# Cross attention's scores as three products of high and low parts, and the memory's values in another buffer

## The reference, cut to what matters

```python
kv = (mem @ mem_w_kv).astype(jnp.float32)
mem_k = kv[..., :D_MODEL].reshape(B, MEM_LEN, XATTN_HEADS, XATTN_HD)   # 4 heads of 256
mem_v = kv[..., D_MODEL:].reshape(B, MEM_LEN, XATTN_HEADS, XATTN_HD)

def memory_cross_attn(x, mem_k, mem_v, wq, wo):
    B, S, _ = x.shape
    q = (x @ wq).reshape(B, S, XATTN_HEADS, XATTN_HD).astype(jnp.float32)
    s = jnp.einsum('bshd,bmhd->bhsm', q, mem_k) * (XATTN_HD ** -0.5)
    p = jax.nn.softmax(s, axis=-1)
    o = jnp.einsum('bhsm,bmhd->bshd', p, mem_v).reshape(B, S, D_MODEL).astype(x.dtype)
    return o @ wo
```

## Time and profile before

| | us |
|---|---|
| median of 3 runs (960.96 to 961.74) | 961.36 |
| the profiled execution, whole | 960.98 |
| its span, first to last instruction | 959.2 |
| PE busy (share of the span) | 945.3 (99%) |
| DVE busy | 685.8 (72%) |
| ACT busy | 518.3 (54%) |
| POOL busy | 54.6 (6%) |
| mean granted TensorE clock, as a share of full speed | 0.997 |

### The profile page before, as it was taken

The page is one execution under the profiler, slowest core; times in us unless marked ns, Lnnn a source line. Parts: engine busy times, 40 slices in busy tenths (PEclk is TensorE's granted clock), DMA queues, the critical chain, the costliest instruction groups (busy, mean ns, idle before and its releaser), DMA issues.

```text
span 959.2 us, 12959 instructions
## 1 busy us (share of the span) xinstructions
PE 945.3 (99%) x5054; PEld 810.4 (84%) x5054; DVE 685.8 (72%) x932; ACT 518.3 (54%) x732; POOL 54.6 (6%) x96
## 2 busy tenths in 40 slices
PE   8999999999999999999999999998999999999996
PEld 8889888888888888888788888887988888888885
DVE  6956578658888775975788777668678886556555
ACT  6756563536655555264275555547465575444543
POOL 0000121001000002100100000002100000000000
PEclk9999999999999999999999999999999999999998
DMA  9975275527988886183289898764631565655521
GB/s 322 337 253 176 88 268 204 209 88 256 338 278 294 283 295 204 52 314 125 88 317 333 271 306 288 249 221 131 229 132 45 176 225 192 219 176 191 178 71 45
DMA packets 110028, 203.00 MB, mean 212 GB/s; under 512 B 4188, under 2 KB 76144, under 8 KB 106640
## 3 DMA queue, kind: packets, MB, share of 16 engines
q1 hardware_dynamic: 106656, 189.67, 58.4%
q0 software_dynamic: 3168, 12.24, 3.7%
q10 hardware_dynamic: 144, 0.26, 0.1%
HBM read 201.09 MB, written 1.06 MB: 211 GB/s over the span
## 4 chain that ended last, share of the span: by engine, by line
PE 90%; DVE 6%; ACT 2%; issue 1%; POOL 0%; DMA 0%; POOLq 0%; SPq 0%; DVEq 0%; ACTq 0%
PE WB L360 20%; PE YB L385 11%; PE YB L378 10%; PE YB L393 10%; PE WB L363 10%; PE YB L439 4%; PE WB L378 2%; PE WB L342 2%; PE WB L385 2%; PE WB L393 2%; PE WB L349 2%; PE WB L345 2%; PE WB L694 1%; PE WB L713 1%; PE WB L477 1%
## 5 line engine op out<-in xcount | busy, mean ns | idle before, releaser
L1709 DVE TENSOR_TENSOR wl<-raw,wh 128x2048 fp32r<-128x2048 f32 (+1 forms) x146 | 334.3, 2297 | 117.4 <-ACT wh L1101 115.1
L1101 ACT CAST wh<-raw 128x2048 fp32r<-128x2048 f32 (+1 forms) x150 | 285.2, 1905 | 30.5 <-PE YB L439 8.9
L360 PE MATMUL WB<-XS,wh 128*128 128x512 f32 x832 | 208.1, 392 | 0.0
L360 PEld LDWEIGHTS WB<-XS,wh 128*128 128x128 f32 x832 | 152.2, 188 | 29.1
L363 PEld LDWEIGHTS WB<-XS,wl 128*128 128x128 f32 x832 | 113.5, 190 | 8.2
L363 PE MATMUL WB<-XS,wl 128*128 128x256 f32 x832 | 116.0, 282 | 0.0
L378 PE MATMUL YB<-wh,FHT 128*128 128x512 f32 x352 | 109.0, 391 | 0.0
L385 PE MATMUL YB<-wl,FHT 128*128 128x512 f32 x352 | 108.6, 390 | 0.0
L393 PE MATMUL YB<-wh,FLT 128*128 128x512 f32 x352 | 108.5, 389 | 0.0
L1275 ACT COPY U<-WB 128x256 f32<-128x256 f32 x102 | 33.0, 376 | 132.8 <-PE WB L363 132.8
L385 PEld LDWEIGHTS YB<-wl,FHT 128*128 128x128 f32 x352 | 66.1, 188 | 14.1
(11 more groups left out here) (338 smaller groups left out, 1205.2 us busy)
## 6 DMA issues: line engine op xcount, KB each, us to landing
raw<-in_mlp_w SPq DMA_DIRECT2D x64, 1024.0 KB, 5.2
raw<-in_w_ada_t SPq DMA_DIRECT2D x24, 1024.0 KB, 5.1
raw<-in_mlstm_w_in SPq DMA_DIRECT2D x11, 1024.0 KB, 8.0
raw<-in_w_ffn_down SPq DMA_DIRECT2D x11, 1024.0 KB, 4.9
raw<-in_w_ffn_gate SPq DMA_DIRECT2D x10, 1024.0 KB, 5.4
raw<-in_w_ffn_up SPq DMA_DIRECT2D x10, 1024.0 KB, 5.6
raw<-in_mem_w_kv SPq DMA_DIRECT2D x8, 1024.0 KB, 5.1
raw<-in_xattn_wq SPq DMA_DIRECT2D x8, 1024.0 KB, 7.2
```

Source lines behind the costliest of these rows:

```text
L360: e.matmul(W[:, :], H[:, at(k)], XS[:, k, :], start=k == 0, stop=False)
L1101: f = e.copy(w[:, 0:a * b], raw[:, 0:a * b])
L1709: f = e.tensor_tensor(L[:, 0:a * b], raw[:, 0:a * b], H[:, 0:a * b].bitcast(F32), ALU.subtract)
```

## The change

Keys are kept as a high part `KH` and a low part `KL_` in a float32r buffer `KHL` (same place in memory as `KV`, which the second block still uses under its own name), queries as high parts in `FH` and low parts in `FL`. `scores(h)` on PE is, for each of the two halves of tokens, two matmuls of high query x high key, two of high x low, and, after a wait for the query's low part, two of low x high. For this

- ACT's copy of a key block becomes a cast into `KH` (same size), and DVE gets four subtractions `key_low(0)` to `key_low(3)`, which now free the key blocks' banks in ACT's place;
- ACT's copies of queries 0 and 1 become casts into `FH`, and for heads 2 and 3 there is a new cast `high(h)`; DVE gets four subtractions `query_low(0)` to `query_low(3)` in each layer;
- the memory's values go to another part of the buffer `AR`, and two vectors (`BV[2]`, `BV[3]`: gain and shift of a later norm) move out of their way; PE's wait for the values moves from `scores` to `values`.

```diff
--- before.py
+++ after.py
@@ -179,13 +179,16 @@
         S = sb("S", [128, 8, 256])
         XS = sb("XS", [128, 8, 512], F32R)
         XH, XL = XS[:, :, 0:256], XS[:, :, 256:512]
+
+        with nc.sbuf_tensor("KHL", [128, 4096], F32R) as KHL:
+            pass
         KV = sb("KV", [128, 4096])
         FHT = sb("FHT", [128, 1280], F32R)
         FLT = sb("FLT", [128, 1280], F32R)
         AR = sb("AR", [128, 8800])
         FH = [FHT[:, 512 * i:512 * i + 512] for i in range(2)]
         FL = [FLT[:, 512 * i:512 * i + 512] for i in range(2)]
-        BV = [sb(f"bv{i}", [128, 1024]) for i in range(2)] + [AR[:, 1024:2048], AR[:, 2048:3072]]
+        BV = [sb(f"bv{i}", [128, 1024]) for i in range(2)] + [AR[:, 4096:5120], AR[:, 5120:6144]]
         IDN = sb("IDN", [128, 128])
         PC = sb("PC", [128, 248])
         SM = sb("SM", [128, 416])
@@ -229,11 +232,11 @@
 
         CT = [S[:, 2 * n:2 * n + 2, :].rearrange("p k c -> p (k c)") for n in range(2)]
 
-        KT = KV[:, 0:2048].rearrange("p (k c) -> p k c", k=8)
-        VM = KV[:, 2048:4096].rearrange("p (t c) -> p t c", t=2)
+        KH, KL_ = (KHL[:, 2048 * n:2048 * n + 2048].rearrange("p (k c) -> p k c", k=8) for n in range(2))
+        VM = AR[:, 2048:4096].rearrange("p (t c) -> p t c", t=2)
 
         TMP = AR[:, 6144:8800]
-        QT = [TMP[:, 512 * n:512 * n + 512] for n in range(2)] + [U[:, 0, 512 * n:512 * n + 512] for n in range(2)]
+        QT = [None, None] + [U[:, 0, 512 * n:512 * n + 512] for n in range(2)]
 
         PART = [U[:, 1, 512 * n:512 * n + 512] for n in range(2)] * 2
         PB = [TMP[:, 1024 + 512 * n:1536 + 512 * n] for n in range(2)]
@@ -686,13 +689,18 @@
 
                 def scores(h):
                     W = bank(("xs", i, h))
-                    e.wait_ge(*act_mlstm["mv", 1, 1])
-                    e.wait_ge(*(act_xa if h < 2 else dve_xa)["q", i, h])
-                    Q = halves(QT[h])
+                    e.wait_ge(*dve_mlstm["mk", 3])
+                    e.wait_ge(*act_xa["qh", i, h])
+                    H, L = halves(FH[h % 2]), halves(FL[h % 2])
                     for t in range(2):
+                        o, tk = W[:, 256 * t:256 * t + 256], slice(128 * t, 128 * t + 128)
                         for f in range(2):
-                            p = e.matmul(W[:, 256 * t:256 * t + 256], Q[:, f, 128 * t:128 * t + 128],
-                                         KT[:, 2 * h + f, :], start=f == 0, stop=f == 1)
+                            e.matmul(o, H[:, f, tk], KH[:, 2 * h + f, :], start=f == 0, stop=False)
+                        for f in range(2):
+                            e.matmul(o, H[:, f, tk], KL_[:, 2 * h + f, :], start=False, stop=False)
+                        e.wait_ge(*dve_xa["ql", i, h])
+                        for f in range(2):
+                            p = e.matmul(o, L[:, f, tk], KH[:, 2 * h + f, :], start=False, stop=f == 1)
                     p.then_inc(pe_xa.add(("s", i, h)))
 
                 def turned(h):
@@ -707,6 +715,7 @@
 
                 def values(h):
                     W = bank(("xv", i, h))
+                    e.wait_ge(*act_mlstm["mv", 1, 1])
                     e.wait_ge(*act_xa["pt", i, h])
                     for d in range(2):
                         for m in range(2):
@@ -720,7 +729,7 @@
                             lambda t, k: e.wait_ge(*dve_xa["o", i, h]))
 
                 def free(t, nb):
-                    return act_xa["q" if t else "ct", i, nb]
+                    return dve_xa["ql", i, nb] if t else act_xa["ct", i, nb]
 
                 s_ = f"wo{i}"
                 pair(s, [("wq", i, 0), ("wq", i, 1)], pe_xa, lambda n: dve_ln["u", s, 0, n])
@@ -1176,8 +1185,7 @@
                 hi_to(M["mk", j] + 3)
                 W = bank_of.get(("mk", j), WB[0])
                 e.wait_ge(*pe_mlstm["mk", j])
-                e.copy(KT[:, 2 * j:2 * j + 2, :], halves(W[:, :])).then_inc(act_mlstm.add(("mk", j)))
-                freed["mk", j] = act_mlstm["mk", j]
+                e.copy(KH[:, 2 * j:2 * j + 2, :], halves(W[:, :])).then_inc(act_mlstm.add(("mk", j)))
 
             def head_a(h):
                 D = DT[h % 2]
@@ -1290,9 +1298,14 @@
                     if h < 2:
                         W = bank_of.get(("xq", i, h), WB[0])
                         e.wait_ge(*pe_xa["xq", i, h])
-                        e.copy(QT[h], W[:, :]).then_inc(act_xa.add(("q", i, h)))
+                        e.copy(FH[h], W[:, :]).then_inc(act_xa.add(("qh", i, h)))
                     else:
                         part(("xq", i, h), PART[h], pe_xa["xq", i, h], act_xa, ("part", i, h))
+
+                def high(h):
+                    e.wait_ge(*dve_xa["q", i, h])
+                    e.wait_ge(*pe_xa["s", i, h - 2])
+                    e.copy(FH[h % 2], QT[h]).then_inc(act_xa.add(("qh", i, h)))
 
                 def scores(h):
                     W, w = bank_of.get(("xs", i, h), WB[0]), cols(("xs", i, h), 6)
@@ -1325,9 +1338,11 @@
                 q(2)
                 hi_to(M["wq", i, 3] + 3)
                 scores(0)
+                high(2)
                 q(3)
                 turned(0)
                 scores(1)
+                high(3)
                 scores(2)
                 values(0)
                 turned(1)
@@ -1855,6 +1870,14 @@
                 decays(h)
                 weighted(h)
 
+            def key_low(j):
+                W = bank_of.get(("mk", j), WB[0])
+                e.wait_ge(*act_mlstm["mk", j])
+                e.tensor_tensor(KL_[:, 2 * j:2 * j + 2, :], halves(W[:, :]),
+                                KH[:, 2 * j:2 * j + 2, :].bitcast(F32), ALU.subtract
+                                ).then_inc(dve_mlstm.add(("mk", j)))
+                freed["mk", j] = dve_mlstm["mk", j]
+
             decays(0)
             decays(1)
             mem_lows()
@@ -1862,14 +1885,18 @@
             weighted(1)
             lo_to(M["mk", 0] + 3)
             lo_to(M["mk", 1] + 3)
+            key_low(0)
             head_c(0)
             lo_to(M["mk", 2] + 3)
+            key_low(1)
             head_a(2)
             head_c(1)
             lo_to(M["mk", 3] + 3)
+            key_low(2)
             head_a(3)
             head_c(2)
             lo_to(M["mv", 0, 1] + 3)
+            key_low(3)
             head_c(3)
             def y_blocks(q):
                 for t in range(2):
@@ -2017,13 +2044,23 @@
                 def query(h):
                     join(("xq", i, h), QT[h], PART[h], act_xa["part", i, h], dve_xa, ("q", i, h))
 
-                for h in range(3):
-                    q(h)
+                def query_low(h):
+                    e.wait_ge(*act_xa["qh", i, h])
+                    e.tensor_tensor(FL[h % 2], QT[h] if h > 1 else YB[2 + h][:, :], FH[h % 2].bitcast(F32),
+                                    ALU.subtract).then_inc(dve_xa.add(("ql", i, h)))
+
+                q(0)
+                query_low(0)
+                q(1)
+                query_low(1)
+                q(2)
                 query(2)
                 scores(0)
                 q(3)
+                query_low(2)
                 query(3)
                 scores(1)
+                query_low(3)
                 scores(2)
                 values(0)
                 scores(3)
```

## The result

The changed kernel takes 969.69 us (median of four runs, 969.03 to 970.11), the kernel before 961.16 (four runs, 960.55 to 961.74): the ratio is 1.0088, with a 95% interval of 1.0076 to 1.0100. It is 8.5 us slower, where 7.2 were forecast. The profiled execution took 970.08, its span 968.2, 9.0 more than before.

A forecast was written before the change was run, and what follows sets the result against it. PE, busy 99% of the span, was taken to bound the kernel. 960.98 plus 4.5 (memory phase) plus 2.74 (cross attention, both layers) gave 968.2 for a profiled-like execution; the median stood 0.38 above, so 968.6 us, range 964.0 to 971.0.

The forecast's parts named there:

- The first hole: Memory phase, before PE's first values matmul: bank WB1 freed late by key_low(2), PE starts at 111.34, not 107.63; 3.7 us.
- The second: Memory phase, before y_turn(0): PE waits for key_low(3) to free WB3, behind two more low parts; 0.77 us more.
- The sum, 4.5: Memory phase: the waits at WB1 and WB3 together, with nothing later giving the time back; +4.5 us.
- Holes of 1.4 and 1.1: Cross attention, each layer: PE waits 1.4 us before scores(2) for head 3's join, 1.1 before values(1) for PT.
- +1.37 forecast: Cross attention, per layer: gains 1.15 us by cheaper scores, loses 2.5 by waits; +2.7 us for both layers.
- The price of the scores: Cross attention on PE: twelve float32r matmuls at 0.12, 1.44 us a head in place of 1.73; 2.3 us won in both layers.
- its fall as a rival: Memory phase: clock falls in the 3.7 us wait, PE then runs at 1.2 GHz; 969.2 to 970.2 us, chance 0.28.
- one fall to go by: End of span: clock falls within 954.0 to 954.5, under 3 us after the last matmul's start, so it may fall mid-kernel.
- the 4.8 us at the start of the span: Start of span: low clock level lasts 4.8 us at most, which would cost 2.4 us in the memory phase, 0.77 free.

The follow-up runs named there:

- the memory's part alone: Changed kernel with queries and scores put back to plain float32 as before the change; key_low and the values' new place stay: 966.93 us, ratio 1.0062.
- one key's low part moved: Changed kernel with only key_low(2) moved on DVE into head_c(1)'s wait for POOL: 970.54 us, ratio 1.0093.
- the other order of cross attention: Changed kernel with DVE's query_low(0) to query_low(2) later and ACT's PT copy of head 1 ahead of head 2's exponential: 965.65 us, ratio 1.0047.

## Why the prediction was right, and its one wrong step

**Direction and place: right.** Of the waits that were forecast, the one at the memory's values and both in each layer of cross attention came in the changed kernel's profile, on the instruction named and released by the one named; the one before the turns came in two experiments. The experiments confirm that order, not quantity, was at fault: the same subtractions cost nothing in the memory phase when they stand in a gap, and with cross attention's order mended too, the whole change costs nothing that the runs can tell.

**The first hole: right.** Forecast 3.7 us, measured 3.68. The second, 0.77, was not seen in the changed kernel's profile but was hidden by the clock's loss; in the two profiles without that loss it came (0.56 and 0.55 in the rows, whose ends include a matmul's depth). The sum, 4.5, was measured as 4.51 in the execution in which the clock stayed.

**Cross attention: right.** Holes of 1.4 and 1.1 were forecast. Rows show 1.09 and 0.94; by the distance of issue the holes are 0.2 longer, 1.3 and 1.1. What counts is the layer: +1.37 forecast, +1.35 and +1.36 measured. The price of the scores was exact, 1.44 us a head.

**The clock: the step that failed.** The forecast took the clock to stay at full in the first hole (chance 0.52) and priced its fall as a rival (0.28, 969.2 to 970.2). It fell in the profile, and the median, 969.69, lies in the rival's range. The price was right in kind: the low level lasted 3.4 us here, not up to 4.8; it cost 1.7 (1.64 in the first eight matmuls, the rest in the next), of which 0.77 was free, so 0.9, and 5.42 - 4.51 = 0.91 was measured. What was wrong was only which case was the likelier one. Four profiles have an unfilled hole of over 3 us: the changed kernel's, the memory's part alone and one key's low part moved, in which the clock fell, and the other order of cross attention, in which it didn't. How often it falls in this hole over many executions isn't known.

Two of the rows on which the forecast weighed the clock say less than it took from them. It had one fall to go by, about 2.3 us behind the last matmul of the span (951.84 to 954.19). The ends of all ten profiles' spans give 2.1 to 5.1 us from the last matmul's end to the fall: five of them 3.2 or less, five 3.7 or more (4.7 in the changed kernel's own). A hole in which PE stands idle for 3.5 us lies in the middle of that spread, so both outcomes were to be expected, and with the same code in the memory phase both came. Which of them an execution gets looks like chance; most of the distance between 968.6 and 969.69 is its price. And the 4.8 us at the start of the span are no upper bound: the changed kernel's execution kept the slow pace until about 9.2 us. The windows of the kernel before give a grant of 1.00 there all the same (2.00 to 4.50), so at the start of a span pace and grant disagree, and the forecast rested on the pace.

The Trainium skill (TensorE: Matmul & The Clock Gate, "Why this matters for your kernels") asks for no long idle gap between bursts of matmuls. Three of four such gaps here agree with it, at 3.5 to 3.8 us in the rows; the fourth, of 3.49 us, doesn't.

**The rest.** 961.16 + 5.42 + 2.71 + 0.13 = 969.4 by the profile's own amounts; 0.3 us to the median are within the spread of runs.

## What to carry to other kernels

Whoever moves the last reader of a bank to another engine gives that engine's whole order a say in when the bank comes free: look up what stands ahead of the new reader, not how busy its engine is. A small instruction that frees something belongs ahead of a long one that frees nothing, or into a gap in which the engine waits anyway. When several banks are freed late, repair all of them; mending the longest wait alone showed only the next one.

## What was not expected of the hardware

The clock fell not in the hole but behind it, when PE was at work again, 3.7 to 4.3 us after the last matmul ahead of the hole had ended (108.55 to 112.22 in the changed kernel): at 112.22 with PE back since 112.06, in the memory-only kernel at 112.54 with PE back since 111.78 (its first matmuls still ran at full), and in the one-key kernel at about 123.66 with PE back since 123.55. And it stayed at half for nearly the same time in all three, about 3.4 us (112.22 to 115.63; 112.54 to 115.95; 123.66 to 127.07, each worked out from a window's mean grant), so that by these three a fall costs a dense PE an estimated 1.7 us:

```profile
123.50:124.00 0.50, 0.45 (x3) 0.48 (x4) 0.41 (x3) 0.00 (x0) 0.00 (x0) 0.66 1.00 410
...
126.00:127.00 1.00, 1.00 (x4) 0.74 (x3) 0.79 (x4) 0.11 (x1) 0.00 (x0) 0.50 0.99 371
127.00:127.50 0.50, 0.50 (x4) 0.40 (x3) 0.00 (x0) 0.50 (x3) 0.00 (x0) 0.93 0.82 311
```
